# Depthwise-convolution taps moved into the input projection, and two TensorE steps moved behind value products, in a decoder layer on one core

## The chip, the cores and the metric

The kernel is one program on one core of a Trainium2 chip. The core has five engines, each with its own in-order instruction stream: TensorE (PE in the profile; PEld are its weight loads) multiplies matrices and transposes, VectorE (DVE), ScalarE (ACT) and GpSimd (POOL) work on elements, and SyncE (SP) issues most DMA transfers. They meet only through semaphores: an instruction that waits holds up everything behind it on its engine. The metric is the device time of one execution in microseconds (us), lower is better.

## The reference, cut to what matters

One layer: a SwiGLU feed-forward, a mixer, a second feed-forward, each followed by a layer norm. There are 256 prompt tokens and 64 sample tokens (8 sequences of 8), 320 in all, of width 1024. The change lies in the mixer:

```python
u = h @ w_in                                  # 1024 -> 2560
q, k, v, ga, gb = split(u);  glu = ga * sigmoid(gb)          # 512 convolution channels
conv = silu(groupnorm(depthwise_conv(glu, width=31) + b_dw)) # channel c: sum over 31 taps
# prompt attention: 8 heads x 256 tokens, causal, ALiBi
# sample attention: of the 8 blocks of 256 cached keys, the 3 with the highest q . mean(k),
#   softmax over these and the own keys, times the cached values
out = concat([attn * beta_attn, conv * beta_conv]) @ w_out
```

The cache is read whole: 32 chunks of keys and 32 of values of about 1 MB each, found through a page table.

## The kernel before, in words

Everything is float32. A product with weights is three TensorE passes (high and low halves of the weights and of the activations); ScalarE rounds a weight unit to its high half and VectorE subtracts to get the low half (`lo`, line 1253; one 128x2048 subtraction per unit, L1255 in the trace).

**Input projection.** `WIN_ORDER` lists ten weight units, each of two 128-column halves: 20 *slots*, numbered 0 to 19. In each slot TensorE runs 24 matmuls of 320 columns, then side work: transposes of tokens in slots 6, 10, 12 and 18, and `prompt_steps(slot)` (line 2175), which carries the eight prompt heads through a short pipeline. `prompt_qk(h)` (L2152, L2153 in the trace) multiplies queries and keys of head h in slot h+10 (h < 4) or h+12; VectorE adds the ALiBi bias and takes maxima (`prompt_scores`, first instruction L1561); ScalarE takes the exponential; VectorE scales (`prompt_probs`, first instruction L1568); TensorE transposes and multiplies by the values one and two slots later. All heads use one accumulator bank, so before head h:

```python
if h:
    pe.wait_ge(ps_ready, h)      # prompt_qk: the scores of head h-1 are out of the bank
```

On VectorE the loop over the slots (line 1572) is written out in program order: the unit's `lo`, the gated product of the convolution (`cbuf`, L1584, in slots 4, 5, 18 and 19), a group of taps in slots 6 and 8, `prompt_probs` of the previous slot's head, `prompt_scores` of this slot's.

**Convolution.** The 512 channels are four chunks of 128. A tap is two instructions, 256 prompt columns and 64 sample columns, added to a running sum. Chunk 0 is VectorE's: `first_taps(a, b)` (line 1553) issues taps a to b-1 through `conv_taps` (L1549 and L1551 in the trace). GpSimd does chunks 1, 2 and 3 one after the other, but `THIRD` taps of chunk 3 are VectorE's.

**Sample attention.** Four pairs of sequences, j = 0 to 3, each of 8 key chunks and 8 value chunks. Keys: TensorE transposes a chunk (L2211), ScalarE and VectorE copy it out (L1116, L1624), TensorE multiplies with the queries (L2236). VectorE reduces the scores and picks blocks (`blocks_chosen`), and TensorE helps with three tiny products that swap numbers between partitions (`parities`, L2267): `gate_sum`, `max_swap` (waits for the block maxima `nmax`) and `prob_sum` (waits for the sums of the exponentials). Then VectorE forms the bias (`bias_ready`), ScalarE takes exponentials, TensorE transposes (L2284). While the softmax of pair j runs, TensorE multiplies the values of pair j-1 (`pair_values`, L2338): `steps` in `next_pair` (line 2378) says behind which of the value chunks 0 to 7 each tiny product stands. Behind chunks 3 and 7 come four products with the own values (L2349). Filler matmuls (`keep_clock`, L2054) stand between some value chunks of the later pairs.

**DMA.** Cache chunks go through ten buffers. SyncE's stream runs over them in order (line 644): wait until the buffer is free, then four page transfers for keys (L488) or three for values (L490, the fourth is ScalarE's). Chunk 3 waits for the low half of the last input unit, chunk 6 for the last slot of the input projection. From chunk 10 a buffer is free when TensorE has transposed or multiplied its last contents; chunk 26 waits for the first value product of pair 0.

Group norm needs the sums of all four chunks: `group_means` stands behind value chunk 6 of the last round.

Of the kernel before, what the change touches and what calls it, by code (L numbers as in the profile page):

```python
# [37 lines left out]
TAPS = 31  # L38
# [78 lines left out]
KVN, KV_RING = 64, 10  # L117
KV_LAST = (0, 1, 2, 3, 4, 5, 8, 9, 0, 1, 4, 5, 2, 3)
ACT_HIGH = (8 + 2, 8 + 5)
THIRD = 6  # L120
ADAN = 9 * D // UC
EARLY = 4
ADA_UP = 2
# [38 lines left out]
def win_kind(u):  # L162

    return max(WIN_ORDER[u] // 2 - 2, 0)
# [7 lines left out]
def head_scored(slot):  # L172

    return slot - 10 if 10 <= slot < 14 else slot - 12 if 16 <= slot < 20 else None
# [93 lines left out]
def build(nc, i, o):  # L268
    es = ExitStack()
    with es:  # L270
# [3 lines left out]
        def sem(name):  # L274
            return es.enter_context(nc.semaphore(name))
# [150 lines left out]
        win_mm, sig_ready, glu_ready, u_out = (sem(n) for n in ("win_mm", "sig_ready", "glu_ready", "u_out"))  # L426
        tok_t, tok_out, st_t, st_in, gl_t, gl_out = (sem(n) for n in ("tok_t", "tok_out", "st_t", "st_in", "gl_t", "gl_out"))
        pad_ready, conv_ready = sem("pad_ready"), sem("conv_ready")
# [284 lines left out]
        def _(pool):  # L713
# [70 lines left out]
            for c in range(1, NCC):  # L784
# [3 lines left out]
                if c == 3:  # L788
                    pool.wait_ge(third_prompt, THIRD)
                    pool.wait_ge(third_sample, THIRD)  # L790
                for k in range(THIRD if c == 3 else 0, TAPS):
                    w = dwT[:, NCC * k + c:NCC * k + c + 1]
# [451 lines left out]
        def _(dve):  # L1244
# [8 lines left out]
            def lo(phase, u, size=NCH * UC, more=0):  # L1253
                dve.wait_ge(w_hi, phase[0] + u + 1 + more)
                dve.tensor_tensor(wl(slot_w(phase, u))[:, 0:size], landed(phase, u)[:, 0:size], wh(slot_w(phase, u))[:, 0:size].bitcast(F32),  # L1255
                                  ALU.subtract).then_inc(w_lo, 1)
# [65 lines left out]
            def samples(ap):  # L1322
                return ap[:, SEQ:T].rearrange("p (b t) -> p b t", b=DB)
# [229 lines left out]
            def first_taps(first, last):  # L1553
                conv_taps(0, first, last, conv_prompt, conv_sample)

            def prompt_scores(h):
                dve.wait_ge(ps_mm, h + 1)
                if h >= 3:
                    dve.wait_ge(pp_t, h - 2)
                sc = ps_[:, h % 3, :]  # L1560
                dve.scalar_tensor_tensor(sc, con[:, C_REL:C_REL + 384], 2.0 ** -(h + 1), bank[:, 6, 0:384], ALU.mult, ALU.add).then_inc(ps_ready, 1)  # L1561
                dve.wait_ge(ps_ready, h + 1)
                dve.tensor_reduce(pm[:, h % 3, 0:1], sc[:, 0:P], AX, ALU.max, negate=True)
                dve.tensor_reduce(pm[:, h % 3, 1:2], sc[:, P:3 * P], AX, ALU.max, negate=True).then_inc(pmax_ready, 1)

            def prompt_probs(h):
                dve.wait_ge(pexp, h + 1)
                link(dve.reciprocal(pr[:, h % 3, :], pz[:, h % 3, :]))  # L1568
                dve.tensor_scalar(ps_[:, h % 3, 0:P], ps_[:, h % 3, 0:P], pr[:, h % 3, 0:1], None, ALU.mult)
                dve.tensor_scalar(ps_[:, h % 3, P:3 * P], ps_[:, h % 3, P:3 * P], pr[:, h % 3, 1:2], None, ALU.mult).then_inc(pp_ready, 1)  # L1570

            for u, b in enumerate(WIN_ORDER):
                for cc in range(2):
                    slot = 2 * u + cc
                    if cc == 0 and 1 <= u < WIN[2] - 3:
                        lo(WIN, u + 2)
                    if cc == 0 and u == WIN[2] - 2:
                        lo(WIN, u + 1)
                    if win_kind(u) == 1:
                        c = 2 * (b - 6) + cc  # L1580
                        dve.wait_ge(*((win_mm, u + 1) if cc == 0 else (w_used, WIN[0] + u + 1)))
                        dve.wait_ge(sig_ready, c + 1)
                        src = bank[:, 2 * (u % 2) + cc, :]
                        dve.tensor_tensor(cbuf[:, c, ST:ST + SEQ], src[:, 0:SEQ], yT[:, c, 0:SEQ], ALU.mult)  # L1584
                        dve.tensor_tensor(cbuf[:, c, ST + SEQ:CB].rearrange("p (b k) -> p b k", b=DB)[:, :, ST:SB],
                                          samples(src), samples(yT[:, c, :]), ALU.mult).then_inc(glu_ready, 1)
                    if slot in (6, 8):
                        dve.wait_ge(glu_ready, 2)
                        dve.wait_ge(st_in, 2)
                        dve.wait_ge(pad_ready, 1)  # L1590
                        first_taps(3 * slot - 18, 3 * slot - 12)
                    if head_scored(slot - 1) is not None:
                        prompt_probs(head_scored(slot - 1))
                    if head_scored(slot) is not None:
                        prompt_scores(head_scored(slot))

            def score_chunk(j, g):

# [15 lines left out]
            def keys_high(j, between={}):  # L1614

                for k in range(8):
                    n = 8 * j + k
                    if n not in ACT_HIGH:
                        dve.wait_ge(kt_ready, 2 * n + 2)
                        if n >= 2:  # L1620
                            dve.wait_ge(k_used, n - 1)
                        if n - 1 in ACT_HIGH:
                            dve.wait_ge(kt_high, n)
                        dve.tensor_copy(kT_view(k, 1), bank_keys(1)).then_inc(kt_high, 1)  # L1624
                    if k in between:
                        between[k]()
                    if k % 2 == 0 and k:
                        score_chunk(j, k // 2 - 1)

            def own_added(j):  # L1630

                s = s_two[j % 2]
                dve.wait_ge(own_ready, j + 1)
                for b2 in range(2):
                    ins = dve.tensor_tensor(s[:, b2, PAST // 2:], bank[:, 6, NS * b2:NS * b2 + NS],
                                            con[:, C_OWN + 56 - DT * (2 * j + b2):C_OWN + 56 - DT * (2 * j + b2) + NS], ALU.add)
                ins.then_inc(own_moved, 1)
# [55 lines left out]
            keys_high(1, {0: first_pair, 1: lambda: blocks_chosen(0), 3: lambda: blocks_added(0, 0), 4: first_bias, 6: lambda: own_added(1), 7: lambda: sums_ready(0)})  # L1693
            for j in range(1, 4):
                if j > 1:
                    between = {6: lambda: own_added(j)}
                    if j == 2:
                        for n, k in enumerate((1, 3, 5, 7)):
                            between[k] = lambda n=n: first_taps(17 + n, 18 + n)
                    keys_high(j, between)  # L1700
                score_chunk(j, 3)
                blocks_chosen(j)
                blocks_added(j, 0)
                bias_ready(j)
                blocks_added(j, 1).then_inc(eb_ready, 1)
                if j < 3:
                    first_taps(*((12, 17), (21, 25))[j - 1])
                else:
                    for c in range(NCC):
                        dve.wait_ge(gm_mm, c + 1)  # L1710
                        y = yT[:, NCC + c, :]
                        dve.tensor_tensor(y, y, bank[:, c, 0:T], ALU.subtract).then_inc(gc_ready, 1)
                sums_ready(j)
                if j == 1:
                    dve.wait_ge(glu_ready, NCC)
                    conv_taps(3, 0, THIRD, third_prompt, third_sample)
                if j == 2:
                    first_taps(25, TAPS)


            dve.wait_ge(gs_ready, 1)
# [25 lines left out]
            for u in range(WOUT[2]):  # L1747
# [3 lines left out]
                for cc in range(2):  # L1751
                    n = 2 * u + cc
# [48 lines left out]
        def _(pe):  # L1801
# [382 lines left out]
            for u in range(2, WIN[2]):  # L2184
                pe.wait_ge(w_lo, WIN[0] + u + 1)
                for cc in range(2):
                    slot = 2 * u + cc
# [84 lines left out]
            def max_swap(j):  # L2272
                parities(nmax_ready, j + 1, C_SWAP, 288, nmax[:, :], 2, swap_mm)

            def prob_sum(j):
                if j == 0:
                    pe.wait_ge(own_moved, 2)
                parities(ex_ready, j + 1, C_SUM, 320, rt[:, :], 2, rsum_mm)
# [99 lines left out]
            def next_pair(j):  # L2378

                if j > 1:  # L2380
                    pair_keys(j)
                steps = {4: lambda: max_swap(j), 7: lambda: prob_sum(j)}
                if j == 1:
                    steps[2] = lambda: own_turned(0)
                if j > 1:
                    steps[0] = lambda: gate_sum(j)
                if j == 3:
                    steps[6] = group_means
                pair_values(j - 1, steps)
                if j == 3:  # L2390
                    group_variances()
                pair_probs(j)
                attn_turn(j - 1)
# [121 lines left out]
```

## Time and profile before

| what | value |
|---|---|
| median of 3 runs | 851.56 us (851.56 to 852.91) |
| the profiled execution | 853.04 us, of which its span is 851.2 us |
| mean granted TensorE clock | 0.995 of full speed |
| PE busy / PEld busy | 96% / 86% of the span |
| DVE, ACT, POOL busy | 55%, 40%, 30% |
| DMA | 197.47 MB, mean 232 GB/s |

The span runs from the first instruction to the last. All positions below are microseconds from its start. The input projection's slots 2 to 19 lie at about 311 to 385, the attention's key and value work at 386 to 572; before and after stand the feed-forwards. A DMA share can read slightly above 1. Busy time of PE counts pipelined matmuls and is no measure of how well it is used; what ends a wait is what tells.

### The profile page before, as it was taken

What the parts mean: (1) busy time and instruction counts of PE and PEld (TensorE: products, weight loads), DVE (VectorE), ACT (ScalarE), POOL (GpSimd) and SP (SyncE); (2) the same over time, 40 slices, a digit from 0 to 9 for tenths busy, and PEclk for the clock granted to TensorE, in tenths of its full rate; (3) what the DMA queues carried; (4) which work ended last, traced back from release to release, by engine and by line L of the source; (5) the groups of instructions that cost most, each with busy time, mean ns of one, the idle gap of its engine ahead of it and who ended that gap; (6) DMA issues with size and microseconds to landing.
All of it is one profiled execution on the core that took longest, in us unless ns stands there. A gap on an engine that the chain in (4) does not pass through costs nothing.

```text
span 851.2 us, 17102 instructions
## 1 busy us (share of the span) xinstructions
PE 818.6 (96%) x6804; PEld 732.7 (86%) x6804; DVE 467.7 (55%) x725; ACT 340.2 (40%) x477; POOL 256.1 (30%) x311
## 2 busy tenths in 40 slices
PE   7999999999999999999998989989999999999997
PEld 6899999999999899887666666559799999999996
DVE  2563643443335678435788987249844444453454
ACT  3253333233223684455354242455753333332240
POOL 2000300000002409999999999102000000000030
PEclk9999999999999999999999999999999999999998
DMA  9997678676955534348999999999244444544421
GB/s 298 349 337 255 221 270 287 232 261 229 355 197 189 167 116 159 98 154 278 374 357 376 335 357 357 354 353 377 86 147 149 149 148 150 179 141 167 136 75 63
DMA packets 159795, 197.47 MB, mean 232 GB/s; under 512 B 12099, under 2 KB 133177, under 8 KB 159717
## 3 DMA queue, kind: packets, MB, share of 16 engines
q1 hardware_dynamic: 150637, 187.94, 65.9%
q10 hardware_dynamic: 8800, 8.43, 3.1%
q8 instruction: 47, 0.77, 0.4%
q0 software_dynamic: 288, 0.14, 0.1%
q14 instruction: 23, 0.19, 0.1%
HBM read 193.67 MB, written 3.17 MB: 231 GB/s over the span
## 4 chain that ended last, share of the span: by engine, by line
PE 75%; SPq 11%; DMA 5%; DVE 4%; issue 2%; ACT 1%; POOL 1%; DVEq 0%; ACTq 0%; POOLq 0%
PE bank L1937 19%; PE bank L1938 18%; PE bank L1939 18%; SPq L490 4%; SPq L488 3%; PE bank L2211 3%; PE bank L1856 3%; DMA raw<-in_ffn_wu 2%; SPq L539 2%; PE bank L2236 2%; DMA araw<-in_w_ada 1%; DMA araw<-in_cache_v 1%; SPq L530 1%; PE bank L1969 1%; PE bank L1963 1%
## 5 line engine op out<-in xcount | busy, mean ns | idle before, releaser
L1255 DVE TENSOR_TENSOR wlo<-raw,whi 128x2048 fp32r<-128x2048 f32 (+1 forms) x72 | 165.2, 2295 | 212.2 <-ACT whi L830 212.2
L1937 PE MATMUL bank<-mh,whi 128*128 128x320 f32 x768 | 239.5, 312 | 0.0
L1938 PE MATMUL bank<-ml,whi 128*128 128x320 f32 x768 | 237.4, 309 | 0.0
L1939 PE MATMUL bank<-mh,wlo 128*128 128x320 f32 x768 | 237.4, 309 | 0.0
L830 ACT CAST whi<-raw 128x2048 fp32r<-128x2048 f32 (+1 forms) x74 | 137.3, 1856 | 195.0 <-PE bank L1939 191.1
L1937 PEld LDWEIGHTS bank<-mh,whi 128*128 128x128 f32 x768 | 144.3, 188 | 5.1 <-issue 5.0
L1938 PEld LDWEIGHTS bank<-ml,whi 128*128 128x128 f32 x768 | 144.3, 188 | 0.1
L1939 PEld LDWEIGHTS bank<-mh,wlo 128*128 128x128 f32 x768 | 144.3, 188 | 0.0
L1937 PE MATMUL bank<-hh,whi 128*128 128x320 f32 x352 | 110.1, 313 | 0.0
L1939 PE MATMUL bank<-hh,wlo 128*128 128x320 f32 x352 | 108.8, 309 | 0.0
L1938 PE MATMUL bank<-hl,whi 128*128 128x320 f32 x352 | 108.8, 309 | 0.0
L720 POOL TENSOR_TENSOR tmp<-yT 128x320 f32<-128x320 f32 x3 | 2.6, 880 | 297.7 <-DVE yT L1348 297.7
L795 POOL TENSOR_SCALAR tmp<-cbuf,dwT 128x256 f32<-128x256 f32 x85 | 86.6, 1019 | 0.1
L802 POOL TENSOR_TENSOR yT<-yT,tmp 128x320 f32<-128x320 f32 x85 | 74.9, 881 | 7.1
L1937 PEld LDWEIGHTS bank<-hh,whi 128*128 128x128 f32 x352 | 66.1, 188 | 3.0 <-issue 2.9
L1938 PEld LDWEIGHTS bank<-hl,whi 128*128 128x128 f32 x352 | 66.1, 188 | 0.2
L1939 PEld LDWEIGHTS bank<-hh,wlo 128*128 128x128 f32 x352 | 66.1, 188 | 0.0
L1116 ACT COPY kT<-bank 128x1024 f32<-128x1024 f32 x32 | 35.7, 1115 | 51.5 <-PE bank L2211 51.5
L903 ACT ACTIVATE tmp<-bank 128x320 f32<-128x320 f32 x44 | 19.0, 437 | 92.8 <-PE bank L1939 91.6
L796 POOL TENSOR_SCALAR tmp<-cbuf,dwT 128x64 f32<-128x64 f32 x85 | 49.4, 582 | 0.0
L1624 DVE COPY kT<-bank 128x1024 f32<-128x1024 f32 x30 | 36.7, 1223 | 20.6 <-PE bank L2211 20.5
L1370 DVE TENSOR_TENSOR tmp<-bank,tmp 128x320 f32<-128x320 f32 x44 | 21.3, 488 | 41.2 <-issue 19.3
(313 smaller groups left out, 1143.4 us busy)
## 6 DMA issues: line engine op xcount, KB each, us to landing
araw<-in_w_ada SPq DMA_DIRECT2D x24, 1024.0 KB, 6.7
raw<-in_ffn_wg SPq DMA_DIRECT2D x19, 1024.0 KB, 8.8
raw<-in_ffn_wu SPq DMA_DIRECT2D x19, 1024.0 KB, 7.0
raw<-in_ffn_wd SPq DMA_DIRECT2D x16, 1024.0 KB, 4.9
raw<-in_cache_k SPq DMA_DIRECT2D x56, 256.0 KB, 4.8
raw<-in_cache_v SPq DMA_DIRECT2D x42, 256.0 KB, 7.1
raw<-in_w_in SPq DMA_DIRECT2D x10, 1024.0 KB, 5.2
aland<-in_w_ada SPq DMA_DIRECT2D x8, 1024.0 KB, 11.2
```

Of the source, the lines that this page charges most:

```text
L488: eng.dma_start(slot[:, 512 * x:512 * x + 512], src.rearrange("a h (g r) d -> (a h g) (r d)", r=8)).then_inc(kv_in[kv_slot(kvi)], 16)
L490: eng.dma_start(slot[x:P:4, :].rearrange("p (h f) -> p h f", h=NH), src.rearrange("a h (g r) d -> g (a h) (r d)", r=4)).then_inc(kv_in[kv_ ...
L795: pool.tensor_scalar(to[:, 0:SEQ], cbuf[:, c, k:k + SEQ], w, *more)
L796: pool.tensor_scalar(to[:, SEQ:T].rearrange("p (b t) -> p b t", b=DB), sam[:, :, k:k + DT], w, *more).then_inc(pool_step, 1)
L802: pool.tensor_tensor(acc_c, acc_c, to, ALU.add).then_inc(conv_ready if last else pool_step, 1)
L830: act.copy(wh(slot_w(phase, u))[:, 0:size], landed(phase, u)[:, 0:size]).then_inc(w_hi, 1)
L1116: act.copy(kT_view(k, 0), bank_keys(0)).then_inc(kt_low, 1)
L1255: dve.tensor_tensor(wl(slot_w(phase, u))[:, 0:size], landed(phase, u)[:, 0:size], wh(slot_w(phase, u))[:, 0:size].bitcast(F32), ALU.subtra ...
L1624: dve.tensor_copy(kT_view(k, 1), bank_keys(1)).then_inc(kt_high, 1)
L1937: pe.matmul(bank[:, b, 0:T], wh(slot)[:, c], h_, start=(start and n == 0), stop=False)
L1938: pe.matmul(bank[:, b, 0:T], wh(slot)[:, c], l_, start=False, stop=False)
L1939: ins = pe.matmul(bank[:, b, 0:T], wl(slot)[:, c], h_, start=False, stop=(stop and n == len(parts) - 1))
```

## The change

Three edits. (1) All 31 taps of chunk 0 are issued by VectorE inside the input projection, 6 each behind slots 6, 8, 11 and 14 and 7 behind slot 17, and behind the slot's `prompt_probs` and `prompt_scores`; the 19 taps that stood in the attention (5 and 14 in pairs 1 and 2) are gone from there. (2) `THIRD` goes from 6 to 10: VectorE takes four more taps of chunk 3, GpSimd four fewer. (3) `max_swap` moves from behind value chunk 4 to behind 6 (pair 2) or 5 (pair 3), and `prob_sum` from behind chunk 7 to behind the own values that follow it.

```diff
--- before.py
+++ after.py
@@ -117,7 +117,8 @@
 KVN, KV_RING = 64, 10
 KV_LAST = (0, 1, 2, 3, 4, 5, 8, 9, 0, 1, 4, 5, 2, 3)
 ACT_HIGH = (8 + 2, 8 + 5)
-THIRD = 6
+THIRD = 10
+TAPS_AT = {6: (0, 6), 8: (6, 12), 11: (12, 18), 14: (18, 24), 17: (24, TAPS)}
 ADAN = 9 * D // UC
 EARLY = 4
 ADA_UP = 2
@@ -1584,15 +1585,15 @@
                         dve.tensor_tensor(cbuf[:, c, ST:ST + SEQ], src[:, 0:SEQ], yT[:, c, 0:SEQ], ALU.mult)
                         dve.tensor_tensor(cbuf[:, c, ST + SEQ:CB].rearrange("p (b k) -> p b k", b=DB)[:, :, ST:SB],
                                           samples(src), samples(yT[:, c, :]), ALU.mult).then_inc(glu_ready, 1)
-                    if slot in (6, 8):
-                        dve.wait_ge(glu_ready, 2)
-                        dve.wait_ge(st_in, 2)
-                        dve.wait_ge(pad_ready, 1)
-                        first_taps(3 * slot - 18, 3 * slot - 12)
                     if head_scored(slot - 1) is not None:
                         prompt_probs(head_scored(slot - 1))
                     if head_scored(slot) is not None:
                         prompt_scores(head_scored(slot))
+                    if slot in TAPS_AT:
+                        dve.wait_ge(glu_ready, 2)
+                        dve.wait_ge(st_in, 2)
+                        dve.wait_ge(pad_ready, 1)
+                        first_taps(*TAPS_AT[slot])
 
             def score_chunk(j, g):
 
@@ -1693,19 +1694,13 @@
             keys_high(1, {0: first_pair, 1: lambda: blocks_chosen(0), 3: lambda: blocks_added(0, 0), 4: first_bias, 6: lambda: own_added(1), 7: lambda: sums_ready(0)})
             for j in range(1, 4):
                 if j > 1:
-                    between = {6: lambda: own_added(j)}
-                    if j == 2:
-                        for n, k in enumerate((1, 3, 5, 7)):
-                            between[k] = lambda n=n: first_taps(17 + n, 18 + n)
-                    keys_high(j, between)
+                    keys_high(j, {6: lambda: own_added(j)})
                 score_chunk(j, 3)
                 blocks_chosen(j)
                 blocks_added(j, 0)
                 bias_ready(j)
                 blocks_added(j, 1).then_inc(eb_ready, 1)
-                if j < 3:
-                    first_taps(*((12, 17), (21, 25))[j - 1])
-                else:
+                if j == 3:
                     for c in range(NCC):
                         dve.wait_ge(gm_mm, c + 1)
                         y = yT[:, NCC + c, :]
@@ -1714,8 +1709,6 @@
                 if j == 1:
                     dve.wait_ge(glu_ready, NCC)
                     conv_taps(3, 0, THIRD, third_prompt, third_sample)
-                if j == 2:
-                    first_taps(25, TAPS)
 
 
             dve.wait_ge(gs_ready, 1)
@@ -2379,14 +2372,16 @@
 
                 if j > 1:
                     pair_keys(j)
-                steps = {4: lambda: max_swap(j), 7: lambda: prob_sum(j)}
+                steps = {4 if j == 1 else 6: lambda: max_swap(j)}
                 if j == 1:
                     steps[2] = lambda: own_turned(0)
                 if j > 1:
                     steps[0] = lambda: gate_sum(j)
                 if j == 3:
+                    steps[5] = lambda: max_swap(j)
                     steps[6] = group_means
                 pair_values(j - 1, steps)
+                prob_sum(j)
                 if j == 3:
                     group_variances()
                 pair_probs(j)
```

VectorE's instructions where slot 11 meets slot 12, before: from the scaling of head 0 (RECIPROCAL) over the scores of head 1 (`ps_`, `pm`) and the low half of unit 8 (`wlo`) to the scores of head 2.

```order
L1568 RECIPROCAL pr<-pz 128x2
L1569 TENSOR_SCALAR ps_<-ps_,pr 128x128
L1570 TENSOR_SCALAR ps_<-ps_,pr 128x256
L1561 SCALAR_TENSOR_TENSOR ps_<-con,bank 128x384
L1563 TENSOR_REDUCE pm<-ps_ 128x1
L1564 TENSOR_REDUCE pm<-ps_ 128x1
L1255 TENSOR_TENSOR wlo<-raw,whi 128x2048
L1568 RECIPROCAL pr<-pz 128x2
L1569 TENSOR_SCALAR ps_<-ps_,pr 128x128
L1570 TENSOR_SCALAR ps_<-ps_,pr 128x256
L1561 SCALAR_TENSOR_TENSOR ps_<-con,bank 128x384
```

The same place in the change, from the scores of head 1 on. Line numbers are one higher; `yT<-cbuf` are taps.

```order
L1562 SCALAR_TENSOR_TENSOR ps_<-con,bank 128x384
L1564 TENSOR_REDUCE pm<-ps_ 128x1
L1565 TENSOR_REDUCE pm<-ps_ 128x1
L1550 SCALAR_TENSOR_TENSOR yT<-cbuf,dwT,yT 128x256
L1552 SCALAR_TENSOR_TENSOR yT<-cbuf,dwT,yT 128x64
...
L1550 SCALAR_TENSOR_TENSOR yT<-cbuf,dwT,yT 128x256
L1552 SCALAR_TENSOR_TENSOR yT<-cbuf,dwT,yT 128x64
L1256 TENSOR_TENSOR wlo<-raw,whi 128x2048
L1569 RECIPROCAL pr<-pz 128x2
L1570 TENSOR_SCALAR ps_<-ps_,pr 128x128
L1571 TENSOR_SCALAR ps_<-ps_,pr 128x256
L1562 SCALAR_TENSOR_TENSOR ps_<-con,bank 128x384
```

Twelve tap instructions (six taps, the first and the last are shown) now stand between the scores of head 1 and the low half of unit 8, ahead of the scores of head 2.

VectorE where slot 17 meets slot 18, before: the scores of head 5, the gated product of chunk 2 (`cbuf`), the scaling of head 5, the scores of head 6.

```order
L1561 SCALAR_TENSOR_TENSOR ps_<-con,bank 128x384
L1563 TENSOR_REDUCE pm<-ps_ 128x1
L1564 TENSOR_REDUCE pm<-ps_ 128x1
L1584 TENSOR_TENSOR cbuf<-bank,yT 128x256
L1585 TENSOR_TENSOR cbuf<-bank,yT 128x8x8
L1568 RECIPROCAL pr<-pz 128x2
L1569 TENSOR_SCALAR ps_<-ps_,pr 128x128
L1570 TENSOR_SCALAR ps_<-ps_,pr 128x256
L1561 SCALAR_TENSOR_TENSOR ps_<-con,bank 128x384
```

The same place in the change.

```order
L1562 SCALAR_TENSOR_TENSOR ps_<-con,bank 128x384
L1564 TENSOR_REDUCE pm<-ps_ 128x1
L1565 TENSOR_REDUCE pm<-ps_ 128x1
L1550 SCALAR_TENSOR_TENSOR yT<-cbuf,dwT,yT 128x256
L1552 SCALAR_TENSOR_TENSOR yT<-cbuf,dwT,yT 128x64
...
L1550 SCALAR_TENSOR_TENSOR yT<-cbuf,dwT,yT 128x256
L1552 SCALAR_TENSOR_TENSOR yT<-cbuf,dwT,yT 128x64
L1585 TENSOR_TENSOR cbuf<-bank,yT 128x256
L1586 TENSOR_TENSOR cbuf<-bank,yT 128x8x8
L1569 RECIPROCAL pr<-pz 128x2
...
L1562 SCALAR_TENSOR_TENSOR ps_<-con,bank 128x384
```

Fourteen tap instructions (seven taps, the first and the last are shown) now stand ahead of the gated product and of everything behind it, among it the scores of head 6.

TensorE in the value products of round j = 2, before: `nmax` is `max_swap`, `rt` is `prob_sum`, `vsam` the own values, `s_even` the transposes.

```order
L2267 MATMUL bank<-nmax,con 128x2 [waits nmax_ready]
L2338 MATMUL bank<-kvw,pT 32x256 [waits kv_in7]
L2338 MATMUL bank<-kvw,pT 32x256 x7
L2338 MATMUL bank<-kvm,pT 32x256 [waits pt_evac,kv_in8]
L2338 MATMUL bank<-kvm,pT 32x256 x7
L2338 MATMUL bank<-kvu,pT 32x256 [waits kv_in9]
L2338 MATMUL bank<-kvu,pT 32x256 x7
L2267 MATMUL bank<-rt,con 128x2 [waits ex_ready]
L2349 MATMUL bank<-vsam,po 32x2x64 [waits pt_evac]
L2349 MATMUL bank<-vsam,po 32x2x64 x3
L2284 MATMUL bank<-con,s_even 128x128 [waits ex_ready]
```

The same place in the change.

```order
L2331 MATMUL bank<-kvw,pT 32x256 [waits kv_in7]
L2331 MATMUL bank<-kvw,pT 32x256 x7
L2331 MATMUL bank<-kvm,pT 32x256 [waits pt_evac,kv_in8]
L2331 MATMUL bank<-kvm,pT 32x256 x7
L2260 MATMUL bank<-nmax,con 128x2 [waits nmax_ready]
L2331 MATMUL bank<-kvu,pT 32x256 [waits kv_in9]
L2331 MATMUL bank<-kvu,pT 32x256 x7
L2342 MATMUL bank<-vsam,po 32x2x64 [waits pt_evac]
L2342 MATMUL bank<-vsam,po 32x2x64 x3
L2260 MATMUL bank<-rt,con 128x2 [waits ex_ready]
L2277 MATMUL bank<-con,s_even 128x128 [waits ex_ready]
```

`max_swap` moved behind two more value chunks, and `prob_sum` behind the four products with the own values; what follows is unchanged.

## Rows read from the trace of the kernel before

**Rows 1.** The page, the chain that ended last: share of the span by engine

```profile
PE 75%; SPq 11%; DMA 5%; DVE 4%; issue 2%; ACT 1%; POOL 1%; DVEq 0%; ACTq 0%; POOLq 0%
```

**Rows 2.** The chain in order of time, attention: start, length, what

```profile
443.46 1.10 PE bank L2338 x16
...
444.72 0.33 SPq L488
...
447.30 1.10 SPq L488
...
489.88 1.42 SPq L488
...
527.87 7.88 DMA raw<-in_cache_v
535.80 1.07 PE bank L2338 x16
```

**Rows 3.** Timeline of DVE, slots 11 and 12: start, length, what [idle before]

```profile
346.38 0.54 DVE L1561 SCALAR_TENSOR_TENSOR ps_<-con,bank 128x384 f32<-128x384 f32 x1
...
347.48 2.28 DVE L1255 TENSOR_TENSOR wlo<-raw,whi 128x2048 fp32r<-128x2048 f32 x1
349.68 0.16 DVE L1568 RECIPROCAL pr<-pz 128x2 f32<-128x2 f32 x1
...
350.37 0.54 DVE L1561 SCALAR_TENSOR_TENSOR ps_<-con,bank 128x384 f32<-128x384 f32 x1
```

**Rows 4.** Timeline of PE: query-key products of heads 3 and 7, first keys

```profile
352.85 0.48 PE L2152 MATMUL bank<-uT 64*128 64x128 f32 x2
...
384.41 0.48 PE L2152 MATMUL bank<-uT 64*128 64x128 f32 x2
...
386.54 1.97 PE L2211 MATMUL bank<-con,raw 128*128 128x128 f32 x16
```

**Rows 5.** Timeline of DVE: taps in slots 6 and 8

```profile
324.58 0.47 DVE L1549 SCALAR_TENSOR_TENSOR yT<-cbuf,dwT,yT 128x256 f32<-128x256 f32 x1
...
325.18 0.47 DVE L1549 SCALAR_TENSOR_TENSOR yT<-cbuf,dwT,yT 128x256 f32<-128x256 f32 x1
...
326.45 0.72 DVE L1549 SCALAR_TENSOR_TENSOR yT<-cbuf,dwT,yT 128x256 f32<-128x256 f32 x1
...
331.64 0.53 DVE L1549 SCALAR_TENSOR_TENSOR yT<-cbuf,dwT,yT 128x256 f32<-128x256 f32 x1
...
336.97 2.28 DVE L1255 TENSOR_TENSOR wlo<-raw,whi 128x2048 fp32r<-128x2048 f32 x1
```

**Rows 6.** Timeline of DVE, slots 15 to 18

```profile
366.17 2.40 DVE L1255 TENSOR_TENSOR wlo<-raw,whi 128x2048 fp32r<-128x2048 f32 x1 [4.66 <-ACT whi L830]
...
379.25 0.41 DVE L1584 TENSOR_TENSOR cbuf<-bank,yT 128x256 f32<-128x256 f32 x1
...
380.87 0.17 DVE L1568 RECIPROCAL pr<-pz 128x2 f32<-128x2 f32 x1 [1.07 <-ACT ps_ L1031]
...
381.82 0.54 DVE L1561 SCALAR_TENSOR_TENSOR ps_<-con,bank 128x384 f32<-128x384 f32 x1
```

**Rows 7.** Waits of PE, 340 to 580: total, times, longest

```profile
PE bank L2236 <- DVE kT L1624: 3.6, 3, 1.3
...
PE bank L2267 <- ACT s_even L1135: 1.1, 1, 1.1
...
PE bank L2267 <- ACT s_odd L1135: 0.8, 1, 0.8
...
PE bank L2267 <- DVE nmax L1663: 0.2, 1, 0.2
```

**Rows 8.** Windows: busy of PE, PEld, DVE, ACT, POOL; clock, DMA share, GB/s

```profile
488.00:492.00 4.00, 3.74 (x62) 1.81 (x58) 3.83 (x12) 0.78 (x1) 3.92 (x5) 1.00 0.92 287
...
500.00:504.00 4.00, 2.88 (x32) 2.14 (x32) 2.81 (x6) 1.32 (x2) 3.83 (x6) 1.00 1.06 397
...
560.00:564.00 4.00, 4.00 (x26) 2.16 (x26) 1.10 (x2) 1.59 (x3) 0.00 (x0) 0.74 1.10 353
```

**Rows 9.** Timeline of PE around its longest wait for a value chunk

```profile
553.59 1.34 PE L2054 MATMUL bank<-con 128*128 128x320 f32 x4
558.24 1.53 PE L2338 MATMUL bank<-araw,pT 128*32 128x256 f32 x16 [3.30 <-DMA araw<-in_cache_v]
559.69 2.50 PE L2054 MATMUL bank<-con 128*128 128x320 f32 x4
```

## The prediction

> **What bounds the kernel now.** I read the page's chain first: three quarters of the span go to TensorE, and 11% to SyncE's queue [rows 1], which is much for an engine that only issues transfers. Then I followed that chain in order of time to see where SyncE comes in [rows 2]. It is TensorE's until the first value product of pair 0, at 443.46. That product frees the buffer for chunk 26, SyncE issues it at 444.72, and the chain stays in SyncE's issues until a value transfer, issued at 527.87, lands 7.88 us later and TensorE takes it at 535.80. So there are three stretches: the input projection and the first two key groups, where TensorE sets the pace; 444 to 528, where SyncE's stream of issues does; and the end of the attention, where TensorE waits for values that land (3.30 us for one of them, [rows 9]). The windows say the same: the DMA share is 0.92 at 488 to 492, so the engines then had room and the issues were late, and 1.06 from 500 on, which is full [rows 8]. A wait of TensorE inside the attention is therefore not on the path, but a delay ahead of 443 is.
>
> Last I read VectorE's and TensorE's timelines side by side in the input projection, since the change adds VectorE work there and VectorE hands TensorE the scores of each head [rows 3 to 6].
>
> **Six taps behind slot 11: a stall.** In before, the scores of head 2 end at 350.37 + 0.54 = 350.91 [rows 3]; TensorE wants them out of the bank for the product of head 3 at 352.85 [rows 4]. The slack is 1.94 us. The change puts six taps ahead of the low half of unit 8 (347.48 in rows 3), the scaling of head 1 and those scores, and these three run without a pause between them, so all of it moves. Six taps took 336.97 - 331.64 = 5.33 us in slot 8 [rows 5], with GpSimd busy beside them as it will be here. TensorE stalls 5.33 - 1.94 = 3.4 us. Queued behind the waiting product are the head steps of slot 13 and every later slot.
>
> Bounds for a tap: the fastest took 325.18 - 324.58 = 0.60 us, a slow one 326.45 - 325.18 = 1.27 [rows 5]. Six are then 3.6 to 7.6 us, the stall 1.7 to 5.7. I take the mean of the six in slot 8 (0.89 a tap): same loop, same neighbours.
>
> **Six taps behind slot 14: no stall.** They meet an idle stretch of 4.66 us ahead of 366.17, in which VectorE waits for ScalarE's rounding of unit 9 [rows 6]. 5.33 us fill it and make the low half 0.7 us late; TensorE needs it only in slot 18, some 10 us on. Cost 0, and 0 at 0.60 a tap; at 1.27 it is 2.9 us late, still inside.
>
> **Seven taps behind slot 17: a second stall.** They take 7 x 0.89 = 6.2 us and stand ahead of the gated product at 379.25. Behind it VectorE had waited 1.07 us for ScalarE, at 380.87, which they eat first. The scores of head 6 ended at 381.82 + 0.54 = 382.36 [rows 6], and TensorE's product of head 7, which needs them, stood at 384.41 [rows 4]: slack 2.05. Stall: 6.2 - 1.07 - 2.05 = 3.1 us (1.1 at 0.60 a tap, 5.8 at 1.27). The gated product of chunk 3 falls behind too, but by less than TensorE.
>
> **Where the stalls go.** The keys start at 386.54 [rows 4]; they will start 6.5 us later. SyncE's loads move with the first stall only, 3.4 us, since they wait for slots 18 and 19; for chunks 16 to 25 the buffers then come free later than SyncE is ready, and chunk 26 waits for the first value product as in before. That is at 443.46 + 6.5, and SyncE's stream behind it moves whole, less the 0.1 us from the product's end (443.46 + 1.10) to the issue at 444.72 that is slack: 6.4. Nothing in the change shortens this stream: its code is the same.
>
> **What the other edits give.** The 19 removed taps and the two moved products aim at TensorE's waits inside the attention: 0.2 us for block maxima, 1.1 and 0.8 for the exponentials, of which the moved products can take back all or part, and 3.6 in three waits for VectorE's copies of keys [rows 7]. Together at most 5.7 us, at least 0. I take 0: all lie behind 443, where the next chunk's issue or landing is late next. The four more taps of chunk 3 cost VectorE 3.6 us (4 x 0.89) just ahead of pair 2's first copy, and five taps, 4.4 us, leave the same place; at worst, if VectorE idles there for the sums, TensorE's wait for that copy grows by the 3.6, and it is hidden for the same reason. GpSimd has four taps fewer; TensorE waits for it nowhere in that view. `max_swap` one chunk later in the last pair makes ScalarE's exponentials some 3 us later (about a value chunk and its filler, 1.10 and 1.34 in rows 2 and 9); the transposes that need them stand two value chunks and the group means further on. Cost 0; if that cover is gone, up to 3.
>
> **The sum.** 3.4 + 3.1 - 0.1 = 6.4 us. Against the profiled execution (853.04: span 851.2 and 1.8 around it) that is 859.4. The profiled execution lies 1.5 above the median of the runs, 851.56; on the median it is 858.0, which I forecast.
>
> **Rivals.**
> *The transfers swallow the second stall.* SyncE's stream has longer issues, 1.10 and 1.42 us against 0.33 (two of five between 447 and 490, [rows 2]); each exceeds the usual by 0.8 to 1.1 us, the five by 4.7. If SyncE is held back there by full DMA engines, it catches up when it is late, and the end moves only as much as the first loads did: 3.4, so 855.0 (at 0.60 a tap 1.7, so 853.3). For it: the share of 1.06 [rows 8]. Against: 0.92 at 488 to 492, where one of the long issues stands while the engines had room. The Trainium skill, page "DMA: Bandwidth & Descriptors", section "Issuing engines are not separate DMA queues", says that a sequencer's time to initiate a DMA is usually small relative to the DMA itself; by that rule the engines bind and not the issues, and this rival would hold. The trace agrees from 500 on, and not at 488 to 492.
>
> *The clock falls in the stalls.* After the 3.30 us wait the granted clock is 0.74 of full speed over 560 to 564 [rows 8], a mix of the two levels 2.4 and 1.2 GHz, and the value product takes 1.53 us against 1.07 in rows 2, the filler 2.50 against 1.34 [rows 9]: 0.46 + 1.16 = 1.6 us. If both stalls, nearly as long, do the same, 3.2 more: 861.2. Against it: these stalls come out of dense products, that one followed a filler of 1.34 us. The Trainium skill, page "TensorE: Matmul & The Clock Gate", section "What's actually happening", says the slow clock is the default and activity lifts it, so an idle engine falls back; the trace agrees at 558, and no row shows it for a stall inside the input projection.
>
> *Faster.* TensorE's own work, not the loads, sets the attention's end: then the waits of rows 7 come back, 5.7 us, and with taps at 0.60 the stalls cost 2.8; 851.56 - 2.9 = 848.7. It decides from where the copies and exponentials end later than the chunks land. For it: TensorE waits for VectorE at all behind 444. Against: the chain does not pass through one of these waits [rows 2].
>
> *No change.* Taps at 0.60 and the transfers recover their 4.7 us: the stalls, 2.8, vanish; 851.6.
>
> **How the numbers follow.** About 0.2% (1.7 us) is what a measurement of this kernel can tell from no change. Forecast 0.55 (own range 855.5 to 860.5); transfers swallow the second stall 0.21; clock 0.08; faster 0.08; no change 0.08. Slower is the sum of the first three, 0.84. The range runs from the low end of the second case, 853.3, to 861.0, near the clock case; of the tap's upper bound (863.0) it leaves out the part in which every tap is as slow as the slowest.
>
> **What would show it.** In the changed profile: a wait of TensorE of about 3 us for VectorE's scores ahead of the products of heads 3 and 7, about 352.9 and 387.8; keys starting near 393; the first value product near 450; the chain again in SyncE's issues behind it; and waits for exponentials and key copies shorter without the end moving. I am wrong if those two products do not wait, or if they wait and the value at 535.80 is taken less than 5 us later.

## The result, and the profile of the changed kernel

The changed kernel takes 862.65 us (median of 6 runs, 860.58 to 866.10), the kernel before 851.47 beside it: 1.3% slower, a ratio of 1.0131 with a 95% interval of 1.0114 to 1.0147. I had forecast 858.0 and a range up to 861.0. The sign and the two stalls came as forecast; the size did not, 11.2 us where I had 6.4. The profiled execution took 862.09 us, its span 860.3.

The chain that ended last, from the page of the changed kernel, against [rows 1]:

```profile
PE 80%; DVE 9%; DMA 3%; SPq 3%; ACT 2%; issue 2%; POOL 1%; DVEq 0%; ACTq 0%; POOLq 0%
```

SyncE's queue has fallen from 11% to 3%, and VectorE has risen from 4% to 9%. TensorE's timeline of the changed kernel (start, length, what, idle before) at the places of [rows 4], with head 4's product and the second key group; the lines of the code have moved, L2145 is the query-key product (here of heads 3, 4 and 7), L2204 the transposes of keys:

```profile
356.65 0.49 PE L2145 MATMUL bank<-uT 64*128 64x128 f32 x2 [2.67 <-DVE ps_ L1562]
...
372.79 0.49 PE L2145 MATMUL bank<-uT 64*128 64x128 f32 x2
...
391.60 0.48 PE L2145 MATMUL bank<-uT 64*128 64x128 f32 x2 [3.31 <-DVE ps_ L1562]
394.18 3.13 PE L2204 MATMUL bank<-con,raw 128*128 128x128 f32 x16
...
398.37 1.97 PE L2204 MATMUL bank<-con,raw 128*128 128x128 f32 x16
```

These are the two forecast stalls, 2.67 and 3.31 us, each for VectorE's scores. The row below the second was not forecast: the first key transposes take 3.13 us, against 1.97 in [rows 4]. The windows of the changed kernel, columns as in [rows 8], say why:

```profile
352.00:356.00 4.00, 1.98 (x14) 1.72 (x12) 3.96 (x8) 0.44 (x1) 3.92 (x4) 1.00 0.00 0
356.00:360.00 4.00, 3.35 (x21) 2.68 (x22) 2.85 (x10) 1.35 (x5) 3.83 (x6) 1.00 0.84 261
...
392.00:396.00 4.00, 4.00 (x21) 3.17 (x21) 3.11 (x9) 1.35 (x5) 3.83 (x6) 0.65 0.93 314
396.00:400.00 4.00, 4.00 (x33) 3.66 (x32) 2.04 (x4) 2.86 (x7) 3.92 (x6) 0.92 0.96 343
```

The granted clock holds at 1.00 behind the first stall and is 0.65 behind the second, a mix of full speed (2.4 GHz) and half (1.2 GHz). Further on, where I had costed the other edits at nothing, two waits have grown (VectorE's copy ahead of pair 2's first keys, and the sums of pair 2's exponentials, against 1.07 for the same product in before):

```profile
472.14 1.97 PE L2204 MATMUL bank<-con,araw 128*128 128x128 f32 x8 [3.25 <-DVE kT L1625]
...
506.44 0.59 PE L2260 MATMUL bank<-rt,con 128*128 128x2 f32 x2 [2.03 <-ACT s_even L1136]
```

So one execution offers two accounts of the missing 5 us: the clock behind the stalls (theory A, later C), or the new waits inside the attention (theory B).

### The profile page after: what moved, and what is told of

Its sections match the earlier page's. It is cut to its first block, busy times and chain, and to the rows that moved or that the text cites. A ratio compares the mean times of both kernels' runs of the same rounds, so it can differ in the third digit from the quotient of the medians.

```text
span 860.3 us, 17104 instructions
## 1 busy us (share of the span) xinstructions
PE 822.9 (96%) x6804; PEld 737.6 (86%) x6804; DVE 472.6 (55%) x733; ACT 339.9 (40%) x477; POOL 248.3 (29%) x299
## 4 chain that ended last, share of the span: by engine, by line
PE 80%; DVE 9%; DMA 3%; SPq 3%; ACT 2%; issue 2%; POOL 1%; DVEq 0%; ACTq 0%; POOLq 0%
PE bank L1930 18%; PE bank L1932 17%; PE bank L1931 17%; PE bank L2204 6%; PE bank L2229 3%; PE bank L1849 3%; PE bank L2331 3%; SPq L540 2%; DMA araw<-in_w_ada 1%; DVE kT L1625 1%; SPq L531 1%; PE bank L1962 1%; DVE yT L1550 1%; DVE yT L1552 1%; PE bank L1956 1%
## 5 line engine op out<-in xcount | busy, mean ns | idle before, releaser
L796 POOL TENSOR_SCALAR tmp<-cbuf,dwT 128x256 f32<-128x256 f32 x81 | 83.1, 1025 | 0.1
L803 POOL TENSOR_TENSOR yT<-yT,tmp 128x320 f32<-128x320 f32 x81 | 76.8, 948 | 6.7
L797 POOL TENSOR_SCALAR tmp<-cbuf,dwT 128x64 f32<-128x64 f32 x81 | 42.9, 530 | 0.0
```

Of the source, the lines that this page charges most:

```text
L796: pool.tensor_scalar(to[:, 0:SEQ], cbuf[:, c, k:k + SEQ], w, *more)
L797: pool.tensor_scalar(to[:, SEQ:T].rearrange("p (b t) -> p b t", b=DB), sam[:, :, k:k + DT], w, *more).then_inc(pool_step, 1)
L803: pool.tensor_tensor(acc_c, acc_c, to, ALU.add).then_inc(conv_ready if last else pool_step, 1)
```

## The experiments

Each time stands beside runs of the kernel before on the same chip.

**The taps into idle stretches.** The stalls are taken away and all else stays.

```diff
-TAPS_AT = {..., 11: (12, 18), 14: (18, 24), 17: (24, TAPS)}
+TAPS_AT = {..., 10: (12, 18), 14: (18, 24), 16: (24, TAPS)}
```

> The changed kernel with the taps of slot 11 issued behind slot 10 and those of slot 17 behind slot 16, where VectorE idles 5.27 and 6.35 us in the kernel before; the same 31 taps in the same order. Theory A (the two stalls of TensorE in the input projection, 2.7 and 3.3 us, and the low clock after the second, 1.6, move the end in full): the products of heads 3 and 7 no longer wait, and the time falls by 7.6 us, from 862.6 to about 855. Theory B (TensorE's later waits in the attention make the end, and absorb the first two): the two products no longer wait either, but the time falls by 3 us at most, to 859.5 or more.

852.99 us, before 852.21, ratio 1.0004 (0.9992 to 1.0016). The whole loss is gone, more than either theory had asked. This *gap version* is the measure for all that follows. Its TensorE rows at the same products and at the first two key groups, from an execution of 855.55 us, the second slowest of its twelve:

```profile
353.89 0.48 PE L2145 MATMUL bank<-uT 64*128 64x128 f32 x2
...
370.03 0.48 PE L2145 MATMUL bank<-uT 64*128 64x128 f32 x2
...
385.46 0.48 PE L2145 MATMUL bank<-uT 64*128 64x128 f32 x2
387.59 1.97 PE L2204 MATMUL bank<-con,raw 128*128 128x128 f32 x16
390.62 1.97 PE L2204 MATMUL bank<-con,raw 128*128 128x128 f32 x16
```

No wait, no slow row. In the attention it has much the same long waits as the changed kernel, though, and a clock of 0.50 behind the first of them (0.61 in the changed kernel):

```profile
463.51 1.97 PE L2204 MATMUL bank<-con,araw 128*128 128x128 f32 x8 [2.42 <-DVE kT L1625]
...
499.23 0.38 PE L2260 MATMUL bank<-rt,con 128*128 128x2 f32 x2 [1.98 <-ACT s_even L1136]
...
503.97 1.97 PE L2204 MATMUL bank<-con,raw 128*128 128x128 f32 x16
...
561.11 1.07 PE L2331 MATMUL bank<-araw,pT 128*32 128x256 f32 x16 [1.53 <-DMA araw<-in_cache_v]
...
569.30 1.07 PE L2331 MATMUL bank<-raw,pT 128*32 128x256 f32 x16
```

```profile
464.00:468.00 4.00, 4.00 (x27) 2.40 (x27) 1.23 (x1) 0.00 (x0) 3.83 (x6) 0.50 1.07 366
```

They cost TensorE some microseconds there: pair 3's first keys start at 503.97, in the kernel before at 497.98, 6.0 later, while the very first keys were 1.1 later. But the value product that waited 3.30 us for its chunk in [rows 9] now waits 1.53, and the last value product is at 569.30 against 568.04. The late TensorE catches up with loads that had not landed anyway. Theory B, that these waits make the loss, falls.

**The other two edits, undone and alone.** Six taps of the last chunk in place of ten; TensorE's products back; those products alone on the kernel before.

```diff
-THIRD = 10
+THIRD = 6
```

> The changed kernel with six taps of the last chunk on VectorE in pair 1 in place of ten, and so GpSimd with four more, as before the change. Theory A: VectorE's copy ahead of pair 2's first key group comes some 3 us sooner, but the end hangs on the loads behind it, 862.6 within 1. Theory B: that copy (3.25 us of wait at 472) is on the path, the low clock behind it too; the time falls by 3 to 4 us, to about 859.

865.69 us, ratio 1.0148 (1.0127 to 1.0168): nothing gained. The wait of 3.25 us is gone from its trace, and TensorE's waits for VectorE ahead of key transposes have fallen from 4.3 us in all to 0.9; but those for value loads have risen from 0.9 to 6.0.

```diff
-                steps = {4 if j == 1 else 6: lambda: max_swap(j)}
+                steps = {4: lambda: max_swap(j), 7: lambda: prob_sum(j)}
...
-                    steps[5] = lambda: max_swap(j)
...
-                prob_sum(j)
```

> The changed kernel with TensorE's two small products (block maxima, probability sums) back where they stood before the change; VectorE's order stays changed. Theory A: nothing, 862.6 within 1. Theory B: in pair 2 the exponentials start some 3 us sooner, the wait of 2.03 us at 506 and the clock of 0.50 behind it go; the time falls by 3 to 5 us, to 858 to 860. If the two moves give back waits as they aim to, it is slower, 863 to 865.

865.51 us, ratio 1.0136 (1.0112 to 1.0159): nothing gained either. The same edit the other way round, on the kernel before:

> The kernel before with the two moves of TensorE's small products and nothing else. Theory A and my prediction: 0, 851.5 within 1. Theory B: the later block maxima make the exponentials of pair 2 late as in the changed kernel; 853 to 855. If the moves take back waits of TensorE (0.2, 1.1 and 0.8 us) and those set the end: 849.5 to 850.5.

852.67 us, ratio 1.0003 (0.9989 to 1.0016): no difference. The loss hangs on neither edit. The first two kernels still have both stalls, and their profiles a lower clock than the changed kernel's own; here, of the one with six taps, the first stall and the windows behind it:

```profile
358.13 0.79 PE L2145 MATMUL bank<-uT 64*128 64x128 f32 x2 [4.35 <-DVE ps_ L1562]
```

```profile
356.00:360.00 4.00, 1.87 (x6) 1.22 (x7) 2.84 (x9) 0.98 (x4) 3.92 (x5) 0.50 0.53 156
360.00:364.00 4.00, 4.00 (x16) 3.34 (x15) 1.80 (x5) 0.48 (x1) 3.83 (x6) 0.50 0.32 107
```

Here the clock is at its lower level behind the first stall too, so that became the question.

**One stall at a time.** The changed kernel with one of its two groups moved to the idle stretch.

```diff
-TAPS_AT = {..., 11: (12, 18), 14: (18, 24), 17: (24, TAPS)}
+TAPS_AT = {..., 11: (12, 18), 14: (18, 24), 16: (24, TAPS)}    # the first stall alone
+TAPS_AT = {..., 10: (12, 18), 14: (18, 24), 17: (24, TAPS)}    # the second stall alone
```

> The changed kernel once more, beside the next three on the same chip. 862.6 by its runs so far, up to 865.6 by the two kernels that differ from it in the attention alone and were no better.

> The changed kernel with the taps of slot 17 behind slot 16, those of slot 11 left: the first stall alone. Theory C: a stall of 2.7 to 4.3 us and 0 to 3.6 us of low clock behind it, all carried to the end: 853.0 + 2.7 to 7.9, so 856 to 861. The rival of the prediction, that transfers swallow the second stall: the whole loss is the first, so 862.6 or more.

> The changed kernel with the taps of slot 11 behind slot 10, those of slot 17 left: the second stall alone. Theory C: 3.3 to 4.3 us and 1.6 to 3.2 us of low clock: 853.0 + 4.9 to 7.5, so 858 to 860.5; with the run before it the two losses add up to that of the changed kernel. The rival that transfers swallow the second stall: 853.0 within 1.

| kernel | us | ratio to before (852.35) |
|---|---|---|
| changed, again | 863.66 | 1.0139 (1.0118 to 1.0159) |
| first stall alone | 858.58 | 1.0074 (1.0057 to 1.0091) |
| second stall alone | 858.49 | 1.0068 (1.0043 to 1.0093) |

6.2 and 6.1 us above before, together 12.4, against 11.3 for both at once: the two add up, within their intervals. The rival that transfers swallow the second stall falls here. SyncE's timeline shows why, first the kernel with the second stall alone, then the gap version:

```profile
370.53 1.88 SPq L489 DMA_DIRECT2D raw<-in_cache_k  x4
...
444.06 5.27 SPq L489 DMA_DIRECT2D araw<-in_cache_k  x8
```

```profile
369.68 2.16 SPq L489 DMA_DIRECT2D raw<-in_cache_k  x4
...
437.60 5.20 SPq L489 DMA_DIRECT2D araw<-in_cache_k  x8
```

The first loads go out 0.9 us later, since they wait for a slot ahead of the stall; 70 us on, they are 6.5 us late. From 320 to 600 us SyncE waits 8.1 us in all for buffers that TensorE's key transposes free, against 1.9 in the gap version. Here the loads did not swallow the delay of the engine that empties their buffers.

The Trainium skill, page "DMA: Bandwidth & Descriptors", section "Issuing engines are not separate DMA queues", holds the time to start a DMA to be usually small beside the DMA itself, which would let the engines and not the issues bind. The trace doesn't contradict it (the DMA share is 1.07 in the gap version's window above), but what decided here was when a buffer came free, which that rule leaves aside.

**The stall kept, the clock held.** Filler products ahead of the two waiting ones, eight and then five.

```diff
+                if h in (3, 7):
+                    pe.wait_ge(tok_out, 6 if h == 3 else 8)
+                    keep_clock(4, 8)        # then: 5
                 if h:
                     pe.wait_ge(ps_ready, h)
```

> The changed kernel with eight filler products (128x320, 0.335 us each by the rows of before) into a bank that is free there, ahead of the products of heads 3 and 7: TensorE works through 2.7 us of each stall, and the stalls themselves stay. Theory C (what the loss has above the two stalls, 3 to 6 us, is the clock that falls to 0.50 in them and stays there for 4 to 8 us): the granted clock holds at 1.00 behind both, and the time falls to the gap version's 853.0 plus the stalls, 6.0 to 7.7, so 859 to 861. Rival D (the excess comes from the loads, which are issued later and meet full engines): 862.6 to 865.6 as without the fillers, or up to 1 more.

861.79 us, ratio 1.0115 (1.0098 to 1.0132), above what I expected, though below the changed kernel's 863.66. TensorE's first filler group and the product behind it, then the windows behind both stalls, of the kernel with eight fillers:

```profile
353.27 4.47 PE L2047 MATMUL bank<-con 128*128 128x320 f32 x16
357.67 0.48 PE L2148 MATMUL bank<-uT 64*128 64x128 f32 x2
```

```profile
356.00:360.00 4.00, 4.00 (x21) 2.58 (x20) 2.84 (x10) 1.46 (x5) 3.83 (x6) 1.00 0.80 261
360.00:364.00 4.00, 4.00 (x28) 3.82 (x28) 0.16 (x1) 0.38 (x2) 3.83 (x6) 1.00 0.00 1
...
392.00:396.00 4.00, 4.00 (x22) 2.58 (x22) 3.29 (x11) 1.47 (x5) 3.83 (x6) 1.00 0.78 225
```

The clock held. But a float32 filler stands in the rows as two (x16 for eight): the 0.335 us I had read from [rows 9] is half of one. Eight took 4.47 us, longer than the stalls of 2.5 to 3.4 in the changed kernel's two traces, so they gave back the clock and took time of their own.

> As the fillers before, with five in place of eight ahead of each of the two products. Eight took 4.47 us, more than the stalls they stood in for (2.5 to 3.6 without them), so they lengthened the first by 1.1 and hid what the clock gave back; five take 2.8 us. Theory C (above the stalls, the loss is the low clock behind them): clock 1.00 behind both stalls, the lag at the first value product 6.0 to 6.9 against the gap version (7.8 to 14.4 without fillers, 8.1 with eight), and 859 to 860 us. Rival D (the clock costs nothing in the end): 862 to 864.

860.73 us, ratio 1.0115 (1.0093 to 1.0136), 0.7 above the top of what theory C expected. The five took 2.85 us, a wait of 1.61 was left ahead of head 3's product, and there the clock fell once more (0.69 at 360 to 364). The times of the two filler kernels alone don't separate C from D: their intervals overlap that of the changed kernel. The traces do, up to the second key group, in the table below.

**A smaller dose.** Three of the six taps behind slot 11, three of the seven behind slot 17, the others in the idle stretches.

```diff
+TAPS_AT = {6: (0, 6), 8: (6, 12), 10: (12, 15), 11: (15, 18), 14: (18, 24), 16: (24, 28), 17: (28, TAPS)}
```

> The gap version with three of the six taps back behind slot 11 and three of the seven back behind slot 17. By the prediction's slack (1.94 us ahead of head 3's product, 2.05 and an idle 1.07 ahead of head 7's) and 0.72 to 0.93 us a tap: 2.2 to 2.8 us meet 1.94, a wait of 0.2 to 0.9 us; and nothing at slot 17. So the gap version's time plus at most 1: 852.5 to 854. Rival: a tap in these places costs its whole length, without slack: 5 us more and the clock besides, 857 to 859.

In the profile it came as the slack said: one wait, ahead of head 3's product, and none at head 7's.

```profile
354.57 0.49 PE L2145 MATMUL bank<-uT 64*128 64x128 f32 x2 [0.93 <-DVE ps_ L1562]
```

The time, 854.90 us, ratio 1.0041 (1.0026 to 1.0056), is 0.9 above what I expected. Against the gap version's ratio that is some 3 us for a wait of 0.9; the profiled execution (854.08) shows no fall of the clock, and what the other executions lose is open.

**The taps alone, in the idle stretches.** Edit 1 in this form on the kernel before, `THIRD` and TensorE's products as there.

> The kernel before with only the taps moved, into the idle stretches (behind slots 6, 8, 10, 14, 16): six taps of the last chunk in pair 1 as before, TensorE's two products where they were. If VectorE's time in the attention is worth nothing there, because the loads set its pace: 852.3 within 1, like before. If the taps taken out of it give back TensorE's waits for copies (3.6 us in the rows of before): 849 to 850.

852.81 us, ratio 1.0012 (1.0001 to 1.0024). TensorE's waits in its trace (total, times, longest):

```profile
PE bank L2229 <- DVE kT L1625: 3.4, 3, 1.3
...
PE bank L2204 <- DVE kT L1625: 0.9, 2, 0.4
```

The 3.6 us of [rows 7], ahead of the key-query products (L2236 in before, L2229 here), are still 3.4: the moved taps give almost nothing of it back. The waits for VectorE's copies ahead of key transposes do fall, from 2.8 us in before to 0.9; those for value loads rise from 3.7 to 4.8, and the time does not follow. No kernel here beats the one before.

**Where the lag arises, in each trace.** How much later than in the gap version TensorE starts the products of heads 3, 4 and 7 and the second key group, taken as differences from one to the next (for the changed kernel 356.65 - 353.89 = 2.76 at head 3, and 372.79 - 370.03 = 2.76 at head 4, so nothing between them):

| profiled execution | us | stall 1 | clock 1 | stall 2 | clock 2 | sum |
|---|---|---|---|---|---|---|
| changed | 862.09 | 2.8 | 0.0 | 3.4 | 1.6 | 7.8 |
| changed, again | 862.04 | 2.6 | 3.1 | 2.5 | 1.5 | 9.7 |
| changed, THIRD 6 | 868.37 | 4.2 | 3.6 | 3.5 | 3.2 | 14.5 |
| changed, TensorE's products back | 868.31 | 4.5 | 3.1 | 2.4 | 3.2 | 13.1 |
| first stall alone | 860.50 | 3.4 | 3.1 | 0.0 | 0.0 | 6.5 |
| second stall alone | 861.86 | 0.1 | 0.0 | 3.4 | 3.2 | 6.6 |
| eight fillers | 861.51 | 3.8 | 0.0 | 4.3 | 0.0 | 8.1 |
| five fillers | 860.40 | 4.1 | 1.5 | 2.7 | 0.0 | 8.3 |
| half dose | 854.08 | 0.7 | 0.0 | 0.0 | 0.0 | 0.7 |

"Stall" is the growth up to the waiting product, "clock" that from there to the next place, in which TensorE works and no wait stands that the gap version has not (0.56 us for ScalarE at 365.54). Wherever "clock" is above 1, a window there has a clock below 0.9; with the eight fillers it is 0.0 twice. The mean over the first four rows is 6.5 us of stall and 4.8 of clock, 11.3; these kernels' medians lie 11.2 to 13.5 above those of the kernel before. These are single executions, and the third and fourth took 2.7 and 2.8 us more than their medians.

Most of the sum reaches the end, not always the whole. In the changed kernel the last value product is at 576.92, 7.6 behind the gap version's; with THIRD 6 at 583.38, 14.1 behind; but in the second execution of the changed kernel at 577.04, 7.7 behind, of a sum of 9.7, and with the fillers 6.9 of 8.1 and 6.1 of 8.3. In that second execution the two long waits of the attention are shorter (2.55 and 1.43 us against 3.25 and 2.03): there they took up part of the lag, as theory B had it for all of it.

## Why the prediction was wrong, step by step

- **The first stall, 3.4 us:** right in place and cause; 2.67 in the changed kernel's profile, mainly because its six taps took 4.32 us there:

```profile
348.47 0.48 DVE L1550 SCALAR_TENSOR_TENSOR yT<-cbuf,dwT,yT 128x256 f32<-128x256 f32 x1
...
352.79 2.28 DVE L1256 TENSOR_TENSOR wlo<-raw,whi 128x2048 fp32r<-128x2048 f32 x1
```

  In the kernel with THIRD 6 they took 5.27 (349.00 to 354.27), against my 5.33, and TensorE waited 4.35. Of my slack of 1.94 (taps less wait) 1.65 and 0.92 were left: VectorE's scalings ahead of the scores took up to 0.69 and 1.07 us there, where the same rows took 0.29 to 0.42 in before.
- **Slot 14, nothing:** right; no wait of TensorE there, and the gap version, which keeps that group, loses nothing.
- **The second stall, 3.1 us:** right, 3.31. Over the table's first four rows both stalls make 6.5 us on the mean, as I had it; that it is the same to the tenth is luck, as they lie between 5.1 and 7.7.
- **The stalls move the end whole:** right. One stall alone costs some 6 us, low clock included, at either of the two places. The first value product is at 452.73, I had it near 450, and the one at 535.80 has moved to 548.50. (The slack that I took as 0.1 is 0.16 by [rows 2]; nothing hangs on it.)
- **The other edits, nothing:** right in the sum, wrong in what I said of the place. I expected waits there to shrink; two grew (3.25 and 2.03 us), the chain left SyncE for TensorE and VectorE, and all of it was regained at the last value chunks (against before, 9.3 us late at the first value product, 14.0 at pair 3's first keys, 8.9 at the last value product). The cover was the landing of the loads, as I had put it. The 5.7 us that the edits aimed at [rows 7] did not come back at all: the same waits make 6.0 in the changed kernel (3.6, 2.0 and 0.4, none for block maxima). What they would have been worth is therefore not shown; that other waits of this kind, 1.9 us of them, were worth nothing, the run with the taps alone shows.
- **The step that failed is the clock.** I kept it out of the sum, as a rival of 0.08, on the ground that "these stalls come out of dense products", unlike the one at 558. The runs show it behind stalls out of dense products in seven of the eight cases of the table's first four rows, at 1.5 to 3.6 us each. I had also priced it too low, 1.6 us a fall, from the one at 558 [rows 9]; why it costs more here was not tried by itself. The range's top of 861.0 rested on 3.2 for both; the four traces have 4.8 on the mean, from 1.6 to 6.8. The time came out near the 863.0 that I had for the slowest taps, but the taps were not the reason: in these traces six took 4.3 to 5.3 us and seven 5.9 to 6.6, where the 863.0 needs 7.6 and 8.9.

The Trainium skill, page "TensorE: Matmul & The Clock Gate", section "What's actually happening", which I had cited for that rival, has the slow clock as the default and activity as what lifts it. The traces agree: 0.50 behind a wait of 4.35 us that follows back-to-back products, and 1.00 where fillers stood in the wait's place; but it stayed at 1.00 behind one wait of 2.67 us too.

## What to carry to other kernels

Before extra work goes onto an engine that feeds another, set its length against the slack between its result and the taker, and put it behind the instructions the other waits for and ahead of one that waits anyway: one slot earlier the same taps cost nothing. Price a stall of TensorE as the wait and the low clock behind it. And where work is taken out of a stage, look first at what ends that stage last: here loads, so waits could shrink or grow by microseconds without the end moving.

## What the runs showed of the hardware

The same wait need not have the same price. In two executions of the changed kernel TensorE waited 2.67 us at the same product after the same work; in one the clock stayed at 1.00, in the other the windows behind it read:

```profile
356.00:360.00 4.00, 3.47 (x13) 2.26 (x13) 2.84 (x10) 1.46 (x5) 3.83 (x6) 0.61 0.80 262
360.00:364.00 4.00, 4.00 (x16) 3.90 (x16) 0.22 (x1) 0.00 (x0) 3.88 (x6) 0.54 0.00 1
```

That alone was 3.1 us at head 4's product, though not at the end: the two executions took 862.09 and 862.04 us, as the second had a shorter second stall and shorter waits in the attention. Over many runs the time does go with the granted clock: the six with the second stall alone stand in its order, from 855.46 us at a mean of 0.991 to 862.12 at 0.984, and with eight fillers five runs lie within 861.39 to 863.01, at 0.990 to 0.993. These are means over whole executions; where in them the clock fell is known for the profiled ones alone. What decides it from one execution to the next stays open. The other surprise is the taps: on the same engine, with GpSimd busy beside it each time, six of them took 4.32 us in one execution and 5.27 in another, the difference lying mainly in the 64-column instructions: one of six took 0.90 us in the first, two took 0.89 and 0.96 in the second, the others 0.27 to 0.41.
